# Second block's heads in pairs on array tiles, columns of the modulation by transposes, last normalisation shared with ScalarE

## The chip, the cores and the metric

The kernel runs on one core of one Trainium2 chip. The metric is device time in microseconds (us), from the first to the last instruction with what the runtime adds around them. All data is float32. Where full speed is wanted, a float32 value is split into a leading part in the fp32r format ("lead") and the difference ("rest"), and a product is made as lead·lead + lead·rest + rest·lead, so three fast matmuls stand for one float32 product. Small products (attention, transposes) use plain float32 matmuls.

## What is computed

A first block (one Hyena-and-attention layer, one mLSTM layer), then a second block of two layers, each a mixer of three branches and an MLP, and a last RMS norm. For 256 tokens of width 1024. The parts that this change touches, cut to what matters:

```python
def adaln(cond, w_mod, b_mod):                       # first block
    m = jax.nn.silu(cond) @ w_mod + b_mod            # shift, scale, gate
h = rms_norm(x, g_pre) * (1 + scale) + shift

# second block, per layer: 8 heads of width 64 twice (MoBA branch and MLA branch), causal
s = q @ k.T * scale          # MLA: 96 features per head, MoBA: 64
p = softmax(s + causal)
o = p @ v                    # v: 64 features per head
# retention branch: 4 heads, 64 features for q and k, 128 for v
o = (q @ k.T * decay) @ v;  o = group_norm(o) * silu(gate)
# each branch: y += sigmoid(gate_b) * (o_b @ w_branch_b), then @ w_out, then the MLP
out = rms_norm(x, final_norm)
```

With 256 tokens the block choice of MoBA has one block only, so that both branches are plain causal attention here.

## The kernel before

The program is one instruction stream per engine. Every piece of work is a generator that yields a place (a number) ahead of each step, and `merge` puts the steps of all generators of an engine in order of these places. So the order is written by hand: one unit of place is one quarter-unit of weights, 12 matmuls of 512 columns in the second block's input projection. Each engine then runs its stream strictly in order and waits on semaphores.

**Weights.** All weights stream through a ring of four 1 MB slots. ScalarE makes the lead (`take_lead`, L325), VectorE the rest (`take_rest`, L144), and `Dense` multiplies (`split_matmul`, L171, and `joined_matmul`, L164 and L165). These matmuls fill TensorE; everything else is slipped between them.

**Attention of the second block** (`CausalAttention`, used four times: MoBA and MLA, in two layers). It goes head by head, one head every 1.4 places: `scores` makes two float32 matmuls (128 and 256 columns; L2566, L2567), `maxima` adds the mask and takes the row maxima on VectorE (L2578, L2581), `exps` is on ScalarE (L2591), `turns` transposes three 128x128 blocks of the probabilities (L2602), `copies` brings them to SBUF (ScalarE, L2612), `values` multiplies with the 128x128 probabilities as weights and 64 columns of v moving (L2623 to L2625), and `outs` divides by the row sums on VectorE (L2634, L2638). In MoBA a head's q and k lie on 64 partitions, the even heads on the lower half and the odd ones on the upper. In MLA they lie on 96.
The results of all three branches go to `oa` (tokens on partitions) and are turned again by `o_turn` in six blocks of four transposes, each block with a copy on ScalarE and a subtraction on VectorE into `oT`.

**Retention** has the same shape, with four heads of 64 features (L2670, L2671), and `group_norm` normalises its output on VectorE (L3025 to L3037) while MLA runs.

**Modulation** (`Mods`). Conditions times `w_mod` are made on four column tiles of 32 (L1008), which leaves partial sums on partitions 0, 1, 32, 33, 64, 65, 96 and 97. For shift and scale, `turns` multiplies each 128 columns of these rows by a selection matrix of two columns (`sel`, L1046), which sums the four parts and turns them at once. VectorE adds the biases from PSUM (L1071 to L1073). There are four such chunks of 512 columns for each of the two layers of the first block; the first four stand ahead of the first projection, where TensorE also runs the Hyena filter (L846, L940).

**The end** (`Finish`). The last product comes in four groups. Each is added to x (L3214), squared on ScalarE, multiplied by the gain (L3251) and scaled by the reciprocal root (L3258, L3261) on VectorE, and stored by four DMAs from SyncE's queue (L3267).

## Time and profile before

| | us |
|---|---|
| median of three runs | 1815.84 |
| lowest and highest run | 1814.3, 1822.47 |
| the profiled execution | 1814.24 |
| its span, first to last instruction | 1812.4 |
| TensorE busy | 1763.4 (97%) |
| VectorE busy | 1157.7 (64%) |
| ScalarE busy | 916.4 (51%) |
| mean granted clock | 0.994 |

1.84 us of the profiled execution lie around its span. The span falls into the first block (to about 925 us), the mixer of the second block's first layer (about 925 to 1130), its output and MLP, the second layer (mixer about 1395 to 1567), its MLP, and an end of some 7 us after the last matmul. TensorE's busy time counts overlapping matmuls; so what a piece costs is read from starts: the distance between the start of the matmul before it and the start of the one after it. A plain fp32r matmul of 512 columns starts every 0.23 us, one of 416 columns every 0.19 us.

### The profile page before, as it was taken

How to read it: one execution, taken by the hardware profiler on the slowest of the kernel's cores; microseconds unless marked ns; L12 is line 12 of the kernel's file. 1: busy time of each engine (PE TensorE's matmuls, PEld its weight loads, DVE VectorE, ACT ScalarE, POOL GpSimd, SP SyncE). 2: the span in 40 equal slices, each digit the busy share in tenths (PEclk: the TensorE clock that was granted, in tenths of full speed). 3: DMA queues.
4: the chain of work that ended last, by engine and by line, in shares of the span. 5: the costliest groups of instructions: out<-in, count | busy, mean ns of one | idle time of the engine just before them, and what ended most of it. 6: DMA issues, size and time to landing. Idle time of an engine off the chain costs nothing. (4 is left out here: it accounts for less than half of the span.)

```text
span 1812.4 us, 23043 instructions
## 1 busy us (share of the span) xinstructions
PE 1763.4 (97%) x8648; PEld 1428.6 (79%) x8648; DVE 1157.7 (64%) x2095; ACT 916.4 (51%) x1484; POOL 47.1 (3%) x67
## 2 busy tenths in 40 slices
PE   9999999999998999999999999999999999999998
PEld 4867788777787877777778788788887888778886
DVE  6563466688428457766766675777646666577844
ACT  4333444333336356656656456367535546547743
POOL 0000000000000010000100010000000002000000
PEclk9999999999999999999999999999999999999999
DMA  9556211221335334443544444556555344455562
GB/s 340 190 180 209 93 58 60 69 71 66 122 114 177 114 110 144 146 151 116 171 133 145 140 145 147 185 169 196 192 188 172 125 146 138 166 167 186 186 212 78
DMA packets 116165, 268.27 MB, mean 148 GB/s; under 512 B 5388, under 2 KB 9773, under 8 KB 115864
## 3 DMA queue, kind: packets, MB, share of 16 engines
q1 hardware_dynamic: 111528, 252.52, 42.4%
q0 software_dynamic: 3696, 11.98, 2.1%
q10 hardware_dynamic: 832, 2.30, 0.3%
q8 instruction: 69, 1.13, 0.2%
q14 instruction: 40, 0.33, 0.1%
HBM read 265.66 MB, written 1.13 MB: 147 GB/s over the span
## 5 line engine op out<-in xcount | busy, mean ns | idle before, releaser
L144 DVE TENSOR_TENSOR qw_rest<-weights,qw_lead 128x1024 fp32r<-128x1024 f32 (+2 forms) x428 | 518.6, 1217 | 404.0 <-ACT qw_lead L325 400.7
L325 ACT ACTIVATE qw_lead<-weights 128x1024 fp32r<-128x1024 f32 (+2 forms) x428 | 446.7, 1048 | 468.2 <-PE psum L171 433.8
L171 PE MATMUL psum<-qw_lead,b_h_pair 128*128 128x512 f32 (+1 forms) x960 | 323.1, 400 | 1.7 <-ACT b_mqk L2925 0.9
L171 PEld LDWEIGHTS psum<-qw_lead,b_h_pair 128*128 128x128 f32 x960 | 180.6, 188 | 41.7 <-issue 5.0
L171 PE MATMUL psum<-qw_rest,b_h_pair 128*128 128x512 f32 (+1 forms) x480 | 186.2, 388 | 0.0
L164 PE MATMUL psum<-b_h_pair,qw_lead 128*128 128x512 f32 x512 | 178.3, 393 | 2.0 <-DVE b_h_pair L662 2.0
L171 PE MATMUL psum<-e_h_lead,qw_lead 128*128 128x512 f32 x320 | 141.1, 441 | 1.8 <-DVE e_qT L1441 1.4
L165 PE MATMUL psum<-b_h_pair,qw_rest 128*128 128x256 f32 x512 | 142.6, 279 | 0.0
L171 PE MATMUL psum<-e_h_lead,qw_rest 128*128 128x512 f32 x320 | 125.8, 393 | 0.0
L171 PE MATMUL psum<-e_h_rest,qw_lead 128*128 128x512 f32 x320 | 125.0, 390 | 0.0
L164 PEld LDWEIGHTS psum<-b_h_pair,qw_lead 128*128 128x128 f32 x512 | 95.9, 187 | 24.3 <-DVE b_h_pair L662 2.9
L171 PE MATMUL psum<-qw_lead,o_h_lead 128*128 128x512 f32 x256 | 110.2, 430 | 3.1 <-PEq L118 3.1
L171 PEld LDWEIGHTS psum<-qw_rest,b_h_pair 128*128 128x128 f32 x480 | 90.7, 189 | 14.8
L171 PE MATMUL psum<-qw_lead,o_h_rest 128*128 128x512 f32 x256 | 101.0, 395 | 0.0
L171 PE MATMUL psum<-qw_rest,o_h_lead 128*128 128x512 f32 x256 | 101.0, 395 | 0.0
L171 PE MATMUL psum<-qw_lead,b_upT_rest 128*128 128x512 f32 x256 | 99.6, 389 | 0.0
L171 PE MATMUL psum<-qw_rest,b_upT_lead 128*128 128x512 f32 x256 | 99.6, 389 | 0.0
L171 PE MATMUL psum<-qw_lead,b_upT_lead 128*128 128x512 f32 x256 | 99.6, 389 | 0.0
L165 PEld LDWEIGHTS psum<-b_h_pair,qw_rest 128*128 128x128 f32 x512 | 96.5, 188 | 0.0
L171 PE MATMUL psum<-qw_lead,e_h_lead 128*128 128x512 f32 x224 | 88.5, 395 | 1.1 <-DVE e_qT L1979 1.1
L171 PE MATMUL psum<-qw_lead,e_h_rest 128*128 128x512 f32 x224 | 87.2, 389 | 0.0
L171 PE MATMUL psum<-qw_rest,e_h_lead 128*128 128x512 f32 x224 | 87.2, 389 | 0.0
(485 smaller groups left out, 3102.5 us busy)
## 6 DMA issues: line engine op xcount, KB each, us to landing
weights<-in_w_in SPq DMA_DIRECT2D x48, 1024.0 KB, 5.1
weights<-in_o_w_in SPq DMA_DIRECT2D x32, 1024.0 KB, 5.4
weights<-in_w_mlp_up SPq DMA_DIRECT2D x32, 1024.0 KB, 5.5
weights<-in_w_mlp_down SPq DMA_DIRECT2D x32, 1024.0 KB, 4.9
weights<-in_e_w_in SPq DMA_DIRECT2D x26, 1024.0 KB, 5.1
weights<-in_w_mod SPq DMA_DIRECT2D x24, 1024.0 KB, 7.3
weights<-in_e_w_out SPq DMA_DIRECT2D x8, 1024.0 KB, 4.9
weights<-in_o_w_out SPq DMA_DIRECT2D x8, 1024.0 KB, 4.8
```

What stands on the lines that cost most here:

```text
L144: return eng.tensor_tensor(self.rest[at], src, self.lead[at].bitcast(F32), ALU.subtract)
L164: nc.tensor.matmul(out, lhs[0], pair, start=start, stop=False)
L165: return nc.tensor.matmul(out[:, 0:lead.shape[1]], lhs[1], lead, start=False, stop=stop)
L171: mm = nc.tensor.matmul(out, l, r, start=start and i == 0, stop=stop and i == 2)
L325: self.core.nc.scalar.activation(self.buf.lead[self.at(u)], self.raw(u), ACT.Copy).then_inc(self.lead_ready, 1)
```

## The change

It has six parts.

1. `CausalAttention` works on pairs of heads, one pair every 2.8 places. The scores of both heads are issued alternately, 128 columns of each and then 256 of each. In MoBA the two heads lie on different 64-row halves of the array. In MLA (96 rows) they can't.
2. The probabilities are divided by their sum before the transposes: a new step `norms` on VectorE (L2618, L2621: a reciprocal and two multiplications of 128 and 256 columns per head). `turns` now waits for it.
3. `values` takes v (64 columns) as weights and the turned probabilities as moving data (256 and 128 columns), with the two heads on different 64-column halves of the array. The result comes out already turned; a ScalarE copy and a VectorE subtraction per pair (`leads`, `rests`) write it to `oT`. `o_turn` is left with the two blocks of retention.
4. Retention's scores also go in pairs on 64-row halves. The steps of `group_norm` and of the rotations stand at other places in VectorE's order, between other work.
5. `Mods` turns shift and scale rows with plain transposes (L1051), and a new reduction on VectorE (L1073, `summed`) adds the four parts. The next chunk's transposes now wait for `summed` of the chunk before, since the four transposes fill the bank.
6. `Finish` gives the first of four scalings to ScalarE (`first_scale`) and the third store to ScalarE's queue, and its steps stand in another order.

Beside these, the masks' load for the mLSTM waits for its gate weights' load on GpSimd, and unused semaphores are gone. Before is marked -, after +.

```diff
     def scores(self, pe):
-            if j >= 2:
-                pe.wait_ge(self.negmax, j - 1)
-            q, k, _, _ = self.heads[j]
-            b = self.banks[j % 2]
-            nc.tensor.matmul(ps[:, b, 0:P], q(0), k(P), start=True, stop=True)
-            nc.tensor.matmul(ps[:, b, P:3 * P], q(1), k(2 * P), start=True, stop=True).then_inc(self.scored, 1)
+            else:
+                pe.wait_ge(self.negmax, 2 * j)
+            for t, (lo, hi) in enumerate(((0, P), (P, 3 * P))):
+                for i in range(2):
+                    q, k, _ = self.heads[2 * j + i]
+                    mm = nc.tensor.matmul(ps[:, self.banks[i], lo:hi], q(t), k((t + 1) * P), start=True, stop=True)
+                    if t:
+                        mm.then_inc(self.scored, 1)
...
+    def norms(self, dve):
+        nc = self.core.nc
+        for j, i, h, at in self.singles(1.3, 0.3):
+            yield at
+            dve.wait_ge(self.exped, 2 * h + 2)
+            self.core.dve_chain(dve, nc.vector.reciprocal(self.rec[:, 2 * h:2 * h + 2], self.tot[:, 2 * h:2 * h + 2]))
+            p = self.prob[:, i, :]
+            for t, (lo, hi) in enumerate(((0, P), (P, 3 * P))):
+                last = nc.vector.tensor_tensor(p[:, lo:hi], p[:, lo:hi], self.rec[:, 2 * h + t:2 * h + t + 1].broadcast_to([P, hi - lo]), ALU.mult)
+            last.then_inc(self.prob_ready, 1)
+
     def turns(self, pe):
-        for j, at in self.times(1.6):
+        for j, i, h, at in self.singles(1.8, 0.45):
             yield at
-            pe.wait_ge(self.exped, 2 * j + 2)
+            pe.wait_ge(self.prob_ready, h + 1)
...
     def values(self, pe):
-            nc.tensor.matmul(ps[:, b, 0:w], pt[:, 0:P], v(0), start=True, stop=True)
-            nc.tensor.matmul(ps[:, b, w:2 * w], pt[:, P:2 * P], v(0), start=True, stop=False)
-            nc.tensor.matmul(ps[:, b, w:2 * w], pt[:, 2 * P:3 * P], v(1), start=False, stop=True).then_inc(self.valued, 1)
+            for t in range(LT):
+                for i in range(2):
+                    v, pt = self.heads[2 * j + i][2], self.probT[:, i, :]
+                    mm = nc.tensor.matmul(ps[64 * i:64 * i + 64, self.banks[3], t * P:2 * P], v(t), pt[:, 2 * t * P:(2 + t) * P], start=(t == 0), stop=(t == 1))
+            mm.then_inc(self.valued, 1)
...
-    o_turn = split_turn(T + "ot_", r.oT, blocks, [branch_at - 5.0 + 0.8 * n for n in range(6)], (3, 4, 5, 6), o_ready, lambda pe: mla.wait_all(pe))
+    o_turn = split_turn(T + "ot_", r.low, blocks, [branch_at - 1.8 + 0.8 * n for n in range(2)], (3, 4), o_ready, lambda pe: mla.wait_all(pe))
...
-    gn_at = t0 + 26.4 + 3 * 1.2 + 2.5
+    gn_at = mla_start + 1.65
...
 # Mods.turns, Mods.takes
-                done = sum(2 for z in self.chunks[:i] if z[1] in (2, 3))
+                done = sum(1 for z in self.chunks[:i] if z[1] < 4)
                 if done:
-                    pe.wait_ge(self.mod_ready, done)
+                    pe.wait_ge(self.summed, done)
                 for b in range(4):
-                    o = (4 * j + b) * 2
-                    mm = nc.tensor.matmul(ps[:, self.spread_bank[0], o:o + 2], self.rows[i % len(self.rows)][:, b * P:(b + 1) * P], sel, start=True, stop=True)
+                    mm = nc.tensor.transpose(ps[:, self.spread_bank[0], b * P:(b + 1) * P], self.rows[i % len(self.rows)][:, b * P:(b + 1) * P], self.core.ident[:])
...
+            nc.vector.tensor_reduce(self.columns[:, 8 * j:8 * j + 8].rearrange("p (b s) -> p b s", s=2), parts, AX.X, ALU.add).then_inc(self.summed, 1)
...
 # Finish
+    def first_scale(self, act):
+        yield self.at - 0.2
+        act.wait_ge(self.rec_ready, 1)
+        act.wait_ge(self.gained, 1)
+        o = self.room.out[:, 0, 0:BANK]
+        self.core.nc.scalar.activation(o, o, ACT.Identity, scale=self.rec[:, 0:1]).then_inc(self.first_ready, 1)
```

TensorE in MoBA of the first layer, before: the values of one head and the scores of another (L171 is the projection, `ga` holds probabilities, `b_gates` turned ones, `hT` q and k, `b_mv` v):

```order
L171 MATMUL psum<-qw_lead,b_h_pair 128x416
L2623 MATMUL psum<-b_mv,b_gates 128x64
L2624 MATMUL psum<-b_mv,b_gates 128x64
L2625 MATMUL psum<-b_mv,b_gates 128x64
L2566 MATMUL psum<-hT 128x128
L2567 MATMUL psum<-hT 128x256
L171 MATMUL psum<-qw_lead,b_h_pair 128x512
```

The same place after: scores of a pair, half a quarter-unit of projection, and values of the pair before.

```order
L171 MATMUL psum<-qw_lead,b_h_pair 128x416
L2584 MATMUL psum<-hT 128x128 x2
L2584 MATMUL psum<-hT 128x256 x2
L171 MATMUL psum<-qw_lead,b_h_pair 128x512
L171 MATMUL psum<-qw_rest,b_h_pair 128x512
L171 MATMUL psum<-qw_lead,b_h_pair 128x512 x2
L171 MATMUL psum<-qw_rest,b_h_pair 128x512
L171 MATMUL psum<-qw_lead,b_h_pair 128x512
L2655 MATMUL psum<-b_gates,b_mv 64x256 x2
L2655 MATMUL psum<-b_gates,b_mv 64x128 x2
```

Six matmuls of 64 columns for two heads became four on half the array's columns, 768 columns in all, and the four score matmuls of two heads stand together.

VectorE in MLA of the first layer, before: the maxima of the second head after the group norm's first steps.

```order
L3025 TENSOR_REDUCE small<-b_oa 128x8
L3026 TENSOR_SCALAR small<-small 128x8
L3028 TENSOR_TENSOR b_oa<-b_oa,small 128x2x512
L144 TENSOR_TENSOR qw_rest<-weights,qw_lead 128x1024
L3030 TENSOR_TENSOR hT<-b_oa 128x1024
L2578 ISA ga,small<-psum,ga 128x128
```

After: the norms of the second head of the first pair, five steps of the group norm, and then the maxima of the next pair (L2597).

```order
L2618 RECIPROCAL small<-small 128x2
L2621 TENSOR_TENSOR ga<-ga,small 128x128
L2621 TENSOR_TENSOR ga<-ga,small 128x256
L3061 TENSOR_REDUCE small<-b_oa 128x8
L3062 TENSOR_SCALAR small<-small 128x8
L3064 TENSOR_TENSOR b_oa<-b_oa,small 128x1024
L2827 TENSOR_SCALAR b_gates<-psum,small 128x512
L144 TENSOR_TENSOR qw_rest<-weights,qw_lead 128x1024
L3066 TENSOR_TENSOR hT<-b_oa 128x1024
L3068 TENSOR_REDUCE small<-hT 128x8
L3069 TENSOR_SCALAR small<-small 128x8
L2597 ISA ga,small<-psum,ga 128x128
```

The whole group norm up to its variance now stands between two pairs.

VectorE at the start of the kernel, after, with the waits: the reduction of the first chunk (L1073) stands behind the four scalings of x.

```order
L1172 RECIPROCAL small<-small 128x4 [waits in_rooted]
L1174 TENSOR_SCALAR x_res<-x_res,small 128x1024 [waits dve_step]
L1174 TENSOR_SCALAR x_res<-x_res,small 128x1024 x3
L1073 TENSOR_REDUCE small<-psum 128x8 [waits m0_spread]
L964 COPY hy_F<-psum 128x512 [waits hy_F_done]
L1073 TENSOR_REDUCE small<-psum 128x8 [waits m0_spread]
```

And TensorE there, after; before, the second chunk waited for `m0_rows_out` only.

```order
L1051 MATMUL psum<-ident,e_qT 128x128 [waits m0_rows_out]
L1051 MATMUL psum<-ident,e_qT 128x128 x3
L943 MATMUL psum<-hT,hy_dft 128x512 [waits hy_filt_out]
L943 MATMUL psum<-hT,hy_dft 128x512
L1051 MATMUL psum<-ident,e_qT 128x128 [waits m0_summed,m0_rows_out]
```

TensorE's second set of transposes waits for VectorE's first reduction, which stands behind four operations of 1024 columns.

## Rows read from the trace of the kernel before

**Rows 1.** The page, busy time of TensorE, share of the span, instructions.

```profile
PE 1763.4 (97%) x8648; PEld 1428.6 (79%) x8648; DVE 1157.7 (64%) x2095; ACT 916.4 (51%) x1484; POOL 47.1 (3%) x67
```

**Rows 2.** Busy time of each engine in a stretch of MLA.

```profile
core 0: us, PE busy (x) PEld busy (x) DVE busy (x) ACT busy (x) POOL busy (x), PEclk, DMA share, GB/s
1060.00:1080.00 20.00, 20.00 (x111) 17.11 (x110) 16.36 (x38) 13.65 (x29) 7.02 (x4) 1.00 0.46 139
```

**Rows 3.** TensorE in order of time: start, duration, a MoBA head's scores.

```profile
972.16 0.35 PE L171 MATMUL psum<-qw_lead,b_h_pair 128*128 128x416 f32 x1
972.45 0.48 PE L2566 MATMUL psum<-hT 64*128 64x128 f32 x2
...
973.30 0.46 PE L171 MATMUL psum<-qw_lead,b_h_pair 128*128 128x416 f32 x1
973.59 0.35 PE L171 MATMUL psum<-qw_rest,b_h_pair 128*128 128x416 f32 x1
```

**Rows 4.** TensorE in order of time: an MLA head's values, then another's scores.

```profile
1060.72 0.33 PE L2623 MATMUL psum<-b_mqk,b_gates 128*128 128x64 f32 x2
...
1061.33 0.44 PE L2566 MATMUL psum<-b_mT 96*128 96x128 f32 x2
...
1062.28 0.39 PE L171 MATMUL psum<-qw_rest,b_h_pair 128*128 128x512 f32 x1
```

**Rows 5.** TensorE in order of time: one block of `o_turn`.

```profile
1112.37 0.60 PE L721 MATMUL psum<-ident,b_oa 128*128 128x128 f32 x4
...
1113.04 0.39 PE L171 MATMUL psum<-qw_rest,b_h_pair 128*128 128x512 f32 x1
```

**Rows 6.** TensorE in order of time: the start of the kernel.

```profile
17.23 1.07 PE L1008 MATMUL psum<-weights,cond 128*32 128x512 f32 x8
18.23 1.99 PE L940 MATMUL psum<-hT,hy_dft 128*128 128x512 f32 x4
...
32.19 1.05 PE L1046 MATMUL psum<-small,e_qT 128*128 128x2 f32 x8 [0.57 <-ACT e_qT L1019]
33.11 1.96 PE L940 MATMUL psum<-hT,hy_dft 128*128 128x512 f32 x4
```

**Rows 7.** VectorE in order of time: the start of the kernel.

```profile
31.90 2.74 DVE L1165 TENSOR_SCALAR x_res<-x_res,small 128x1024 f32<-128x1024 f32 x4
```

**Rows 8.** VectorE in order of time: MLA of the first layer.

```profile
1054.04 1.22 DVE L3025 TENSOR_REDUCE small<-b_oa 128x8 f32<-128x1024 f32 x1
...
1063.02 0.16 DVE L2634 RECIPROCAL small<-small 128x2 f32<-128x2 f32 x1
1063.21 0.29 DVE L2638 TENSOR_TENSOR b_oa<-psum,small 128x128 f32<-128x128 f32 x1
1063.42 0.28 DVE L2578 CUSTOM_DVE_ANT_0 ga<-psum,ga 128x128 f32<-128x128 f32 x1
...
1063.62 0.42 DVE L2578 CUSTOM_DVE_ANT_0 ga<-psum,ga 128x256 f32<-128x256 f32 x1
1063.97 0.09 DVE L2578 DVE_READ_ACCUMULATOR2_ANT small<- 128x1 f32 x1
```

**Rows 9.** The two costliest lines of VectorE and ScalarE: busy, mean ns.

```profile
L144 DVE TENSOR_TENSOR qw_rest<-weights,qw_lead 128x1024 fp32r<-128x1024 f32 (+2 forms) x428 | 518.6, 1217 | 404.0 <-ACT qw_lead L325 400.7
L325 ACT ACTIVATE qw_lead<-weights 128x1024 fp32r<-128x1024 f32 (+2 forms) x428 | 446.7, 1048 | 468.2 <-PE psum L171 433.8
```

**Rows 10.** Who waited for whom: total us, times, longest.

```profile
PE psum L2602 <- ACT ga L2591: 0.3, 1, 0.3
```

**Rows 11.** VectorE in order of time: the end.

```profile
1805.19 0.15 DVE L3258 RECIPROCAL small<-small 128x1 f32<-128x1 f32 x1
1805.38 0.48 DVE L3261 TENSOR_SCALAR hT<-hT,small 128x512 f32<-128x512 f32 x1
1805.78 0.74 DVE L3214 SCALAR_TENSOR_TENSOR x_res<-psum,small,x_res 128x512 f32<-128x512 f32 x1
...
1808.84 0.88 DVE L3261 TENSOR_SCALAR hT<-hT,small 128x512 f32<-128x512 f32 x2
```

248 lines of the change are left out of this document (139 added, 109 removed).

## Prediction

> **What bounds the kernel now.** I read the page's busy times first: TensorE is busy for 1763.4 of 1812.4 us, VectorE for 1157.7 [rows 1]. In the mixers of the second block, where most of the change lies, TensorE has no gap in stretches of 20 us, even where VectorE is busiest, at 16.36 of 20 us [rows 2]. So time comes off only where TensorE's stream gets shorter, and a cost on another engine counts only where TensorE then waits. The waits say that this hardly happens now: in the four attentions the transposes of the probabilities waited once for the exponentials, for 0.3 us [rows 10]. Next I read TensorE's order of time around each small piece. A piece costs the distance between the starts of the projection matmuls on either side, less the ordinary distance of these (0.19 us at 416 columns, 0.23 us at 512). All sums are made against the profiled execution's 1814.24 us; the median of the three runs, 1815.84, is 1.6 us above it, and I forecast near the profiled level.
>
> **Scores on row halves.** One MoBA head's two score products take 973.59 - 972.16 = 1.43 us with a 0.19 us step at either end, so about 1.05 us [rows 3]. MoBA has 8 heads in each of two layers, so 8 pairs. If the two halves run side by side, a pair costs what a head costs now, and 8 x 1.05 = 8.4 us go. Bounds: if the halves take turns, only one entry and exit per pair goes, 2 x 1.05 - (1.05 + 0.85) = 0.2 us, as 973.30 - 972.45 = 0.85 is a head without them [rows 3]; that is 1.6 us. If the pair is as well filled as a 96-row head, 62.28 - 61.33 - 0.23 = 0.72 us [rows 4], it is 8 x 1.38 = 11.0 us. I take 8.4. Retention's scores have the same rows, columns and form; 8 heads or 4 pairs give 4.2 us (0.8 to 5.5). MLA's scores keep their columns and don't overlap: nothing.
> No row shows two row halves at once. The nearest are the column tiles of the modulation: four products of 512 columns on four 32-column tiles took 1.00 us until the next matmul started, while two full-array products of that length have 1.99 us [rows 6]. So tiles do run side by side on this chip, in one direction of the array at least. The Trainium skill says the same of both directions (TensorE: Matmul & The Clock Gate, Part 3: Packing small matmuls).
>
> **Values on column halves.** A head's six instructions (three products) take 61.33 - 60.72 = 0.61 us now, 1.22 us a pair [rows 4]. The new form streams 384 columns per head. A float32 product of 384 columns in all costs 0.72 us in MLA's scores [rows 4], so a pair side by side costs about that, and up to 1.05 us if a half-array group has the overhead that the MoBA scores show [rows 3]. I take 0.80: 16 pairs x 0.42 = 6.7 us. Bounds: 16 x 0.17 = 2.7 and 16 x 0.50 = 8.0 us. If they took turns, a pair would cost 1.4 us and the sum would lose 3 us, but the four column tiles speak against that [rows 6].
> A rule of the Trainium skill speaks against this part: a change of the tiling mode drains TensorE (TensorEngine Tiling (Array Packing), Key Properties). The trace bears it out as the difference of 1.05 to 0.72 us between the half-row and the 96-row scores; by the rule alone values would cost 1.05 a pair, which is the lower bound above.
>
> **Fewer transposes.** A block of four costs 1113.04 - 1112.37 - 0.23 = 0.44 us [rows 5]. Four blocks go in each layer: 8 x 0.44 = 3.5 us. Their ScalarE and VectorE work isn't saved, it moves into `leads` and `rests`.
>
> **Modulation.** A chunk's four two-column products take 33.11 - 32.19 = 0.92 us [rows 6], four transposes 0.44 [rows 5], so 0.48 us less per chunk. For the four chunks of the second set, which lie within the projection, that is 1.9 us. In the first set the new wait decides. Before, the second chunk starts at 32.19. Now it needs the first chunk's reduction, and that stands in VectorE's order behind the four scalings of x, which run from 31.90 to 34.64 [rows 7]; with some 0.2 us for a small reduction it starts at about 34.85. It is 2.66 us late and 0.48 shorter: 2.2 us lost, and everything behind it on TensorE moves (filter, transposes of x, the next products), as no gap follows until the first projection. Two more chunks give back 0.96. The set costs 1.2 us; all modulation gains 0.7 (bounds -2 and +3). The reductions themselves are a few tenths on VectorE and hidden by the 8 quarter-units between chunks.
>
> **What the norms add to VectorE.** Now a head's reciprocal and division are 0.19 + 0.21 = 0.40 us from start to start; the new step is a reciprocal, 128 and 256 columns, 0.19 + 0.21 + 0.35 = 0.75 [rows 8]. 32 heads make +11 us, hidden if TensorE doesn't wait. But the chain from scores to transposes gets longer. For an ordinary pair TensorE has 24 projection matmuls (5.5 us), its scores and the values of the pair before, some 7.7 us, ahead of the first transpose. VectorE has ahead of its norm: two maxima (0.77 each), one or two weight rests (1.14 each), a result's rest (0.35) that itself waits for the values, and the norm: it is done some 0.8 us before it is due. The tight place is MLA's second pair, behind the group norm. From the first scores of MLA on, VectorE has 1.5 (maxima) + 1.5 (norms) + 1.14 (rest) + six steps of the group norm (four of 1024 columns at about 1.2, two small: 5.1) + a projection output and a weight rest (1.8) + maxima, weight rest, result (2.3) + maxima and norm (1.5), 14.8 us in all [rows 8, 9]; TensorE comes to that transpose after 4.6 places, 12.7 + 2.6 + 1.4 = 16.7 us. With the waits for the first scores and for exponentials within, that leaves next to nothing. I take one turn late by a norm, 0.75 us, in each of the four attentions: 3 us lost. Bounds: 0, and half a norm for each of 32 turns, 12 us.
>
> **The end.** The fourth addition moves ahead of the first scaling, from 1805.78 to about 1805.3 [rows 11], but ScalarE now has the first scaling ahead of its last two squares, which gives 0.1 or 0.2 us of it back, and the last two scalings stay. The third store leaves SyncE's queue. I take 0.7 us (0 to 1.0).
>
> **Costs that I set at nothing.** The later group norm: GpSimd, which takes it up, then still waits for the gates. The masks' later load: it is issued far ahead of its reader. Rotations in pieces: the same instructions.
>
> **Sum.** 8.4 + 4.2 + 6.7 + 3.5 + 0.7 + 0.7 - 3.0 = 21.2 us, so 1793.0 us.
>
> **Rivals.**
> A. Row halves take turns. Scores then give 1.6 + 0.8 instead of 12.6 us: 1814.2 - 11.0 = 1803.2. For it: no row of before has two row halves in flight. Against it: the column tiles.
> B. VectorE late more often: some 10 to 17 us of new waits, so that most of the gain comes back, 1803 to 1810, with 1807 in the middle. For it: 16.36 of 20 us in rows 2, and the exact fit at the second MLA pair. Against it: VectorE waits for 404 us of the kernel on the line that it spends most time in [rows 9], so it catches up in a pair or two.
> C. Slower: VectorE becomes the bound of the attentions. If each of the 32 transposes of a head waits for its norm and one weight rest queued ahead (0.75 + 1.14 us), 60 us are added and 24 saved, 1850 us. It turns slower than now from 0.76 us of waiting per turn (24.2 / 32).
> D. The change doesn't save on the values, since the halves serialise or each small product pays a full load: 6.7 turns to -3, 1803.
>
> **How the numbers follow.** Forecast 0.57, A 0.12, B 0.14, C 0.06, D 0.05, and 0.06 for a part worth more than I took. The range reaches from 1784 (scores, values and retention at their better bounds and no new wait: 21.2 + 2.6 + 1.3 + 1.3 + 3.0 = 29.4 us) to 1809, which holds A, D and most of B. About 0.5% (9 us) is what a measurement of this kernel can tell from no change, so the line is at 1805: the forecast, what is better than it, A and D lie below it, 0.80, B within 0.5%, 0.14, and C above, 0.06.
>
> **What would show it.** TensorE: MoBA score groups with both heads started within a few hundredths and about 1.05 us for the group; values groups of 0.8 us; 16 transposes fewer per layer; a gap of about 3.5 us near 31 us, ended by the reduction. VectorE: about 1170 us busy. The waits: transposes of the probabilities waiting for L2621, a few times, 3 us together. Wrong would be: score groups of 1.9 us (A), many waits for L2621 or for L144 (B, C), values groups of 1.4 us (D).

## Result and profile after

| | before | after |
|---|---|---|
| median of the runs | 1815.84 | 1804.62 |
| lowest and highest | 1814.3, 1822.47 | 1803.35, 1807.37 |
| profiled execution, its span | 1814.24, 1812.4 | 1805.85, 1803.7 |
| ratio after to before, 95% interval | | 0.994, 0.9929 to 0.9951 |

The changed kernel is faster by 11.2 us (medians), 0.6%. The forecast was 1793.0, a gain of 21.2 us on the profiled execution before, so about half of it came. The measured time alone doesn't tell which rival is right: A (1803.2), D (1803) and the lower end of B (1803 to 1810) lie near it. All times are in us.

The page of the changed kernel, busy time of the two engines of [rows 1]. TensorE has 22 us less to do, near the 24 us that the forecast's terms make without the new waits, and VectorE 12 us more (some 1170 were forecast):

```profile
PE 1741.3 (97%) x8520; PEld 1395.5 (77%) x8520; DVE 1169.8 (65%) x2142; ACT 918.9 (51%) x1493; POOL 47.0 (3%) x67
```

TensorE in order of time, first layer: one pair of MoBA scores (what a single head was in [rows 3]), and one pair of values alone ([rows 4] has one head's):

```profile
968.39 0.34 PE L171 MATMUL psum<-qw_lead,b_h_pair 128*128 128x416 f32 x1
968.67 0.93 PE L2584 MATMUL psum<-hT 64*128 64x128 f32 x8
969.52 0.46 PE L171 MATMUL psum<-qw_lead,b_h_pair 128*128 128x416 f32 x1
969.82 0.35 PE L171 MATMUL psum<-qw_rest,b_h_pair 128*128 128x416 f32 x1
...
1090.89 0.40 PE L171 MATMUL psum<-qw_lead,b_h_pair 128*128 128x512 f32 x1
1091.22 0.87 PE L2655 MATMUL psum<-b_gates,b_mqk 128*64 128x256 f32 x8
1092.02 0.50 PE L171 MATMUL psum<-qw_lead,b_h_pair 128*128 128x512 f32 x1
1092.35 0.40 PE L171 MATMUL psum<-qw_rest,b_h_pair 128*128 128x512 f32 x1
```

969.82 - 968.39 less two steps of 0.19 is 1.05 for two heads: the row halves run side by side. 1092.35 - 1090.89 less two steps of 0.23 is 1.00 for the values of two heads, where 0.80 was forecast and 1.33 was paid before (0.66 to 0.67 a head, read in the same way).

Who waited for whom on TensorE (total, times, longest), the lines that are new or longer than before. Before had L2602 with 0.3 [rows 10]; L171 for the gates' copies had 2.0, once, and L721 (now L724) 0.9, twice:

```profile
PE psum L2632 <- DVE ga L2621: 6.5, 7, 1.3
...
PE psum L171 <- ACT b_gates L2826: 3.3, 3, 2.0
...
PE psum L1051 <- DVE small L1073: 2.4, 1, 2.4
...
PE psum L724 <- ACT hT L2825: 1.7, 2, 0.8
...
PE psum L2632 <- ACT b_gates L2642: 0.7, 3, 0.2
```

A wait isn't all that a stop costs. In MLA of the first layer a group of transposes costs 0.34; the one that waited 0.67 costs 1.22, the one that waited 1.30 costs 1.86. So each stop has 0.2 us on top.

### The profile page after: what moved, and what is told of

It is laid out like the page before. It is cut to its first block and busy times, and to the rows that moved or that the text cites. A ratio compares the mean times of both kernels' runs of the same rounds, so it can differ in the third digit from the quotient of the medians.

```text
span 1803.7 us, 22788 instructions
## 1 busy us (share of the span) xinstructions
PE 1741.3 (97%) x8520; PEld 1395.5 (77%) x8520; DVE 1169.8 (65%) x2142; ACT 918.9 (51%) x1493; POOL 47.0 (3%) x67
## 5 line engine op out<-in xcount | busy, mean ns | idle before, releaser
L171 PE MATMUL psum<-qw_lead,b_h_pair 128*128 128x512 f32 (+1 forms) x960 | 320.5, 399 | 3.2 <-ACT b_gates L2826 1.4
L171 PEld LDWEIGHTS psum<-qw_lead,b_h_pair 128*128 128x128 f32 x960 | 181.0, 189 | 43.7 <-issue 3.7
L171 PE MATMUL psum<-qw_rest,b_h_pair 128*128 128x512 f32 (+1 forms) x480 | 186.5, 389 | 0.0
L171 PE MATMUL psum<-e_h_lead,qw_lead 128*128 128x512 f32 x320 | 141.1, 441 | 1.8 <-DVE e_qT L1450 1.4
L171 PE MATMUL psum<-e_h_lead,qw_rest 128*128 128x512 f32 x320 | 125.8, 393 | 0.0
L171 PE MATMUL psum<-e_h_rest,qw_lead 128*128 128x512 f32 x320 | 124.9, 390 | 0.0
L171 PE MATMUL psum<-qw_lead,o_h_lead 128*128 128x512 f32 x256 | 109.6, 428 | 3.1 <-PEq L118 3.1
L171 PEld LDWEIGHTS psum<-qw_rest,b_h_pair 128*128 128x128 f32 x480 | 90.7, 189 | 14.9
L171 PE MATMUL psum<-qw_lead,o_h_rest 128*128 128x512 f32 x256 | 100.6, 393 | 0.0
L171 PE MATMUL psum<-qw_rest,o_h_lead 128*128 128x512 f32 x256 | 100.5, 392 | 0.0
L171 PE MATMUL psum<-qw_lead,b_upT_rest 128*128 128x512 f32 x256 | 99.6, 389 | 0.0
L171 PE MATMUL psum<-qw_rest,b_upT_lead 128*128 128x512 f32 x256 | 99.6, 389 | 0.0
L171 PE MATMUL psum<-qw_lead,b_upT_lead 128*128 128x512 f32 x256 | 99.6, 389 | 0.0
L171 PE MATMUL psum<-qw_lead,e_h_lead 128*128 128x512 f32 x224 | 88.5, 395 | 1.1 <-DVE e_qT L1988 1.1
L171 PE MATMUL psum<-qw_lead,e_h_rest 128*128 128x512 f32 x224 | 87.2, 389 | 0.0
L171 PE MATMUL psum<-qw_rest,e_h_lead 128*128 128x512 f32 x224 | 87.2, 389 | 0.0
```

Of the source, the lines that this page charges most:

```text
L171: mm = nc.tensor.matmul(out, l, r, start=start and i == 0, stop=stop and i == 2)
```

## Experiments

The table holds every kernel's median, its ratio to the kernel before (95% interval), and four lengths from its one profiled execution: the start of the first projection matmul; the first layer's MoBA stage, from its first scores to the first retention scores; and the MLA stage of both layers, from its first scores to the first branch matmul. The lengths tell causes apart that the medians can't: where a kernel leaves a stage alone, its length comes back within 0.1 (MoBA 57.41 in before and 57.43 in `e_mods`). The first projection doesn't: it lies between 53.3 and 55.7 in the kernels that differ from the changed one only behind it. Three lengths also hold a fall of the granted clock to 0.50 behind a wait, which cost 1.6 each time: MoBA of `e_low_place`, and MLA of `e_lnexp` in both layers.

| kernel | median | ratio | first projection | MoBA | MLA, layers 1, 2 |
|---|---|---|---|---|---|
| before | 1815.84 | | 50.92 | 57.41 | 76.46, 77.44 |
| after | 1804.62 | 0.994 | 53.55 | 53.71 | 76.67, 77.61 |
| e_pairs | 1806.57 | 0.9943 (0.9929, 0.9958) | 51.35 | 54.35 | 76.45, 77.47 |
| e_mods | 1817.61 | 1.0004 (0.9994, 1.0015) | 55.09 | 57.43 | 76.51, 77.45 |
| e_no_norm | 1802.13 | 0.9921 (0.9906, 0.9936) | 55.67 | 52.50 | 75.79, 76.74 |
| e_norm_twice | 1815.46 | 0.999 (0.9981, 0.9998) | 54.43 | 56.31 | 79.09, 80.07 |
| e_low_place | 1807.96 | 0.9957 (0.9941, 0.9972) | 54.41 | 55.59 | 76.70, 77.68 |
| e_lnexp | 1812.03 | 0.9976 (0.9966, 0.9986) | 54.68 | 53.63 | 78.92, 80.12 |
| e_no_norm_lnexp | 1806.7 | 0.995 (0.9935, 0.9965) | 53.93 | 52.64 | 77.25, 78.21 |
| e_no_root | 1804.95 | 0.9934 (0.9921, 0.9948) | 55.07 | 51.81 | 76.68, 77.64 |
| e_early_tables | 1803.66 | 0.9929 (0.9914, 0.9943) | 53.30 | 52.27 | 76.72, 77.67 |
| e_values_one_half | 1812.7 | 0.9981 (0.9973, 0.9989) | 54.11 | 55.79 | 78.19, 79.11 |
| e_reduce | 1802.43 | 0.9926 (0.9912, 0.994) | 50.21 | 53.71 | 76.71, 77.68 |
| e_norm_first | 1805.76 | 0.994 (0.9928, 0.9952) | 54.73 | 53.25 | 76.57, 77.53 |
| e_gn_late | 1805.42 | 0.994 (0.9928, 0.9952) | 54.27 | 53.69 | 76.65, 77.57 |
| e_finish_old | 1805.06 | 0.9939 (0.9927, 0.9951) | 55.29 | 53.66 | 76.68, 77.63 |
| e_best1 | 1798.73 | 0.9909 (0.9894, 0.9924) | 50.29 | 51.39 | 76.33, 78.12 |
| e_best3 | 1795.78 | 0.9889 (0.9874, 0.9904) | 54.34 | 51.40 | 74.86, 76.58 |
| e_best4 | 1795.15 | 0.9886 (0.987, 0.9903) | 51.08 | 51.41 | 74.88, 76.58 |

### Are the parts worth what was forecast?

My first theory was that the parts on TensorE are right and the missing 10 us are transposes that wait for VectorE. `e_pairs` is the kernel before, with the paired scores alone:

```diff
-            nc.tensor.matmul(ps[:, b, 0:P], q(0), k(P), start=True, stop=True)
-            nc.tensor.matmul(ps[:, b, P:3 * P], q(1), k(2 * P), start=True, stop=True).then_inc(self.scored, 1)
+            for t, (lo, hi) in enumerate(((0, P), (P, 3 * P))):
+                for i in range(2):
+                    q, k, _, _ = self.heads[2 * n + i]
+                    mm = nc.tensor.matmul(ps[:, self.banks[i], lo:hi], q(t), k((t + 1) * P), start=True, stop=True)
```

> The kernel before with one part of the change alone: MoBA's and retention's scores in pairs on 64-row halves. The prediction put 8.4 + 4.2 = 12.6 us on it, so 1803.2 against 1815.8. The groups of the changed kernel read 1.05 us a pair as forecast, so I expect 11 to 13 us. Rival: a pair frees TensorE but the head behind waits for its maxima or its decay, since two heads come at once (VectorE then has two heads' maxima in a row, the second head's exponentials wait); then 7 to 9 us, 1807 to 1809.

Ratio 0.9943, 10.3 us by it, between the two forecasts. A pair costs 1.05, as forecast; retention's stage loses 1.98 per layer (2.1 forecast). MoBA gains 3.06 in the first layer instead of 4.2, since a value product of the old form waits 2.02 us for the division of the head before; in the kernel before it waited 1.04 at the same place. VectorE and, last, TensorE there:

```profile
994.72 1.22 DVE L2529 TENSOR_TENSOR b_gates<-hT,x_res 128x1024 f32<-128x1024 f32 x1
...
998.51 0.29 DVE L2654 TENSOR_TENSOR b_oa<-psum,small 128x128 f32<-128x128 f32 x1
998.95 0.41 PE L2639 MATMUL psum<-b_mv,b_gates 128*128 128x64 f32 x2 [2.02 <-DVE b_oa L2654]
```

The division stands behind the four steps of a rotation (L2529 to L2532, 994.72 to 998.41), and not behind maxima. So row halves side by side are shown; the rival is right that a stop takes some of it back, and not in its reason.

`e_values_one_half` is the changed kernel, with both heads' values on one column half:

```diff
-            for t in range(LT):
-                for i in range(2):
+            for i in range(2):
+                for t in range(LT):
                     v, pt = self.heads[2 * j + i][2], self.probT[:, i, :]
-                    mm = nc.tensor.matmul(ps[64 * i:64 * i + 64, self.banks[3], t * P:2 * P], v(t), pt[:, 2 * t * P:(2 + t) * P], start=(t == 0), stop=(t == 1))
+                    mm = nc.tensor.matmul(ps[0:64, self.banks[3], SEQ * i + t * P:SEQ * i + 2 * P], v(t), pt[:, 2 * t * P:(2 + t) * P], start=(t == 0), stop=(t == 1))
```

> The changed kernel with the value products of both heads of a pair on the same 64-column half, one head after the other, into different columns of the bank (the odd heads' outputs then don't reach their rows, that part of the computation is wrong on this run): same number of products, columns and weights, no two side by side. The groups of two heads take 1.00 us in the changed kernel. If the halves overlap, the columns alone (768 of float32, 1.05 us for 384 in a half-row group, 0.72 in MLA's) make this 1.6 to 1.9 us a pair, 16 pairs, 10 to 14 us more, 1814 to 1819. Rival D of the prediction (the halves take turns or each product pays its load anyway): the same 1.00 us, 1804 to 1806.

A pair costs 1.64 to 1.66 instead of 1.00, and the kernel 7 to 8 us more, less than the 10 to 14 expected. So the column halves do overlap, for 0.65 us of each pair, and rival D is out. (16 x 0.65 is 10.4. The stages grow by 2.1 in MoBA and 1.5 in MLA, 7.1 in both layers; part of the rest is waits that are shorter, as the transposes behind now come later: 4.7 us for L2621 instead of 6.5.)

### The start

`e_mods` is the kernel before with the new `Mods` alone, `e_reduce` the changed kernel with one step elsewhere (x's norm stands at places -14.95 and -14.6):

```diff
-            yield self.turn_at[i] + self.lags[2] - self.lags[1]
+            yield self.first_sum if i == 0 and self.first_sum else self.turn_at[i] + self.lags[2] - self.lags[1]
...
+    mods0.first_sum = -14.96
```

> The kernel before with one part of the change alone: the modulation's shift and scale by plain transposes and a reduction. The prediction gives it 0.7 us of gain (second set 1.9 less, first set 1.2 more), 1815.1. The changed kernel's trace has the second set at -1.9, and the first set at +2.6 to the first projection, but its start was also disturbed by a wait for a load and by the clock. If the loss of 2.6 belongs to the change, this kernel is 0.7 us slower than before, 1816.5; if it is the run's, it is 0.7 to 1.8 faster, 1814 to 1815.1.

> The changed kernel with one step at another place: the first chunk's reduction of the modulation goes ahead of VectorE's normalisation of x instead of behind its four scalings. In the kernels with the changed modulation TensorE stops for 4.6 to 4.9 us there (L1051 waits for L1073), in the matmuls behind the stop the four of L943 take 3.6 instead of 1.9 us, and the first projection comes at 55.1 to 55.7 against 50.9 before. Theory (the wait and the clock behind it cost 4 us): first projection at about 50 to 51, 4 to 5 us less than the changed kernel, 1800 to 1801. Rival (x's scalings bound the start anyway, since TensorE's transposes of x need them all): TensorE stops there instead, 1 to 2 us less, 1802.6 to 1803.6.

`e_mods` isn't faster, 1.0004: its first projection comes 4.2 us later than before, and the four chunks of the second set give 1.9 back. TensorE in order of time in `e_no_norm` (same start), and the busy times of engines in two stretches of it (the column before DMA's share is the granted clock, PEclk):

```profile
28.78 0.66 PE L1051 MATMUL psum<-ident,e_qT 128*128 128x128 f32 x4
29.27 1.88 PE L943 MATMUL psum<-hT,hy_dft 128*128 128x512 f32 x4
35.75 1.09 PE L1051 MATMUL psum<-ident,e_qT 128*128 128x128 f32 x4 [4.60 <-DVE small L1073]
36.63 3.62 PE L943 MATMUL psum<-hT,hy_dft 128*128 128x512 f32 x4
```

```profile
core 0: us, PE busy (x) PEld busy (x) DVE busy (x) ACT busy (x) POOL busy (x), PEclk, DMA share, GB/s
28.00:32.00 4.00, 3.15 (x16) 1.07 (x8) 0.17 (x1) 3.63 (x8) 0.00 (x0) 1.00 1.05 388
...
36.00:40.00 4.00, 4.00 (x8) 1.88 (x8) 1.10 (x8) 0.00 (x0) 0.00 (x0) 0.50 0.45 164
```

The transposes are done at 29.3, but the reduction stands in VectorE's order behind x's norm, which waits for ScalarE's squares of x. After the stop of 4.60 the granted clock is 0.50, that is 1.2 of 2.4 GHz, and the same four matmuls take 3.62 instead of 1.88. The changed kernel's own profiled run had a wait of only 2.44 and kept its clock behind it. TensorE came late to it there, since it had waited 1.71 us for a load (L849) at 12.83 and had a granted clock of 0.50 from 15.0 to 21.5. With the reduction ahead of x's norm the first projection comes at 50.21 and the median is 2.2 us lower, less than the theory's 4 to 5: TensorE now waits 1.7 us at the same chunk for ScalarE's copy, which stands behind the same squares.

`e_best4` took that copy away too (with all other remedies, below):

> The version with all remedies, and the copy of the modulation's second chunk made by VectorE, ahead of x's norm, instead of by ScalarE behind x's squares and root. Theory (x's scalings, which end at 34.6 us, are the third in the same row and TensorE's transposes of x need all four): the 1.7 us wait at the second chunk goes, TensorE then stops about as long ahead of the transposes of x, the first projection stays at about 50 us and the time within 1 us of the last version, 1795 to 1796.5. Rival (the copy was the last thing in the way): the first projection comes 1.7 us earlier, 1794.

```profile
31.52 0.60 PE L1052 MATMUL psum<-ident,e_qT 128*128 128x128 f32 x4
31.96 1.88 PE L943 MATMUL psum<-hT,hy_dft 128*128 128x512 f32 x4
35.48 1.09 PE L1186 MATMUL psum<-ident,x_res 128*128 128x128 f32 x8 [1.64 <-DVE x_res L1175]
```

As expected: the stop moves to the transposes of x, 1.64, and the first projection stays near, at 51.08. The start is bound by x's load and norm. `e_best3` shows the load: it has the early reduction too, but the third of ScalarE's four squares, which waits for the load of x in both, starts at 29.82 instead of 27.48 in `e_reduce`. TensorE waited 4.36 for ScalarE's copy, the granted clock fell to 0.50 behind it, and the first projection came at 54.34. So the place of the reduction doesn't take the stop away in every execution.

### MoBA: who makes the transposes wait?

`e_no_norm` and `e_norm_twice` take VectorE's new work away and double it (the diff of the first; the second repeats the loop over `t`):

```diff
-        self.vector, self.scalar = (self.maxima, self.norms, self.rests), (self.exps, self.copies, self.leads)
+        self.vector, self.scalar = (self.maxima, self.rests), (self.exps, self.copies, self.leads)
...
-            pe.wait_ge(self.prob_ready, h + 1)
+            pe.wait_ge(self.exped, 2 * h + 2)
```

> The changed kernel without its step `norms`: the transposes wait for the exponentials, the probabilities are not divided by their sums (that part of the computation is left out), and VectorE has 0.9 us less to do for each of 32 heads, some 28 us in all. The changed kernel took 1804.6. My theory now: the missing 10 us of the forecast lie mainly in transposes that wait for VectorE (17.4 us of PE's and the weight loader's idle time stand under L2632 and L2621, over about ten turns, and a turn that waits costs its wait and about 0.5 us more). Then this kernel takes 8 to 10 us less than the changed one, 1795 to 1797. Rival 1, the prediction's own figure: the waits cost 3 us, so 1801 to 1802. Rival 2: TensorE stops elsewhere for the same VectorE work (projection groups, value groups), so that nothing is gained, 1804.

> The changed kernel with the two multiplications of each head made twice (the probabilities are divided by their sum two times, so the attention outputs are not the reference's): VectorE has about 0.7 us more per head, 22 us in all, on the chain ahead of each transpose. If the transposes wait because VectorE is late, most heads become late ones: each head that already waits adds 0.7 us, and others begin to wait at 0.5 us for the stop itself; 32 heads, some 10 to 20 us more, 1815 to 1825. Rival (only a few places are tight, the others have slack of a microsecond or more): 10 waiting turns by 0.7 us, 7 us, 1811 to 1813.

My theory fell with the first. Without norms only 3.4 us come back by the ratio (0.9921 against 0.994; 2.5 by the medians), because the transposes then wait for ScalarE. Its waits, first line:

```profile
PE psum L2632 <- ACT b_gates L2642: 5.2, 8, 1.1
```

Twice the norms cost 9 us by the ratio (11 by the medians), with 16 waits of 16.8 us in all, as its theory said. So VectorE matters, but it isn't the only one that is late. ScalarE of the changed kernel in order of time, at MoBA's second pair, and below it VectorE's norm for it (it is ready for the transpose at 986.08, which waited 0.85):

```profile
980.95 0.39 ACT L2662 ACTIVATE b_oT_lead<-psum 128x256 fp32r<-128x256 f32 x1 [2.13 <-PE psum L2655]
981.35 1.28 ACT L2941 ACT_TABLE_LOAD   x1
982.65 0.21 ACT L2941 ACTIVATE small<-small 128x4 f32<-128x4 f32 x1
982.87 1.28 ACT L2610 ACT_TABLE_LOAD   x1
984.17 0.40 ACT L2610 ACTIVATE ga<-ga,small 128x128 f32<-128x128 f32 x1
```

```profile
985.19 0.17 DVE L2618 RECIPROCAL small<-small 128x2 f32<-128x2 f32 x1 [1.92 <-ACT ga L2610]
985.39 0.63 DVE L2621 TENSOR_TENSOR ga<-ga,small 128x128 f32<-128x128 f32 x2
```

VectorE had been idle for 1.92 us. The exponentials were late because ScalarE loaded a table for the square root of `low_root` and another to come back: 2.8 us with the root. Four kernels test this: the root at its old place (1.0 instead of 0.55), the roots as exp(-0.5 ln x), that without norms, and copies in place of the roots; `e_early_tables` puts the loads into ScalarE's idle time:

```diff
-        yield low_at + 0.55
+        yield low_at + 0.4
         act.wait_ge(low_meaned, 1)
         nc.scalar.activation(r.low_stat[1], r.low_stat[0], ACT.Sqrt).then_inc(low_rooted, 1)
+        yield low_at + 0.6
+        nc.scalar.activation(core.small[:, 60:61], core.small[:, 60:61], ACT.Exp)
```

> The changed kernel with one line back at its old place: ScalarE's root of the MLA inputs' norm (`low_root`, place 0.55) at place 1.0 again. In the changed kernel this root brings two loads of activation tables (1.28 us each, 2.8 us with the root) between the maxima and the exponentials of MoBA's second pair, and the norms and transposes behind them are those that wait at 986.08 and 989.08. Theory (ScalarE's tables are what the waits named after VectorE's L2621 hide): both waits of MoBA go in each layer, so 2.5 to 4 us less than the changed kernel, 1800.6 to 1802. Rival (VectorE is loaded in MoBA whatever ScalarE does): the waits stay, within 1 us of 1804.6.

> The changed kernel with both square roots inside the attentions (MLA inputs' norm and group norm) made as exp(-0.5 ln x), whose two functions can share one table with the exponentials, so that no table is loaded between them (four loads of 1.28 us fewer per layer). Theory (ScalarE's tables): the waits at 986, 989 and 1076 of the first layer and 1420 and 1509 of the second go; with about 0.5 us for each stop saved too, 4 to 6 us less than the changed kernel, 1798.6 to 1800.6. What stays by this theory is the transpose at 1067.33 (1.30 us), whose norm stood behind a weight rest that waited for ScalarE's lead. Rival (VectorE's own work): same waits, 1803 to 1805.

> Both at once: without the norms (the probabilities are not divided, that part of the computation is left out) and with the roots as exp(-0.5 ln x). Leaving out the norms alone gave 1802.1, since the transposes then waited 5.2 us for ScalarE's copies (L2642) in place of 7 us for the norms. Theory (behind both names stands ScalarE, late by its table loads): now neither is late and nearly nothing waits, 1795 to 1798. Rival (a transpose group has only one PSUM bank, so the second head's transposes wait for the first head's copy whatever ScalarE has before it): the waits for copies stay, 1800 to 1802.

> The changed kernel with plain copies in place of the two square roots inside the attentions (MLA inputs' norm and group norm; that part of the computation is left out), so that ScalarE loads no table there: four loads of 1.28 us fewer per layer are possible, and this time the trace can show it, which the exp(-0.5 ln x) form did not (it loaded a table for each of its two functions, back to back, and the MLA stage became 2.3 us longer per layer). Theory (ScalarE's loads are behind most waits): waits of the transposes fall from 7.2 to about 1.5 us (the one at 1067 stays in each layer), 4 to 6 us less than the changed kernel, 1798.6 to 1800.6. Rival: VectorE's own load makes them, 1803 to 1805.

> The changed kernel with ScalarE's table loads at better places and nothing left out: the root of MLA's inputs goes ahead of the copy that waits for the first pair's values (ScalarE is idle for 2.1 us there), and an exponential of a single element behind each root brings the table back before the maxima are ready. Theory: the exponentials of MoBA's second pair and MLA's third come 1.3 us earlier each, and about half of the transposes' waits go: 2 to 3.5 us less than the changed kernel, 1801 to 1802.6. Rival: the loads only move ahead of other work that is waited for (copies of probabilities, leads), 1804 to 1806.

- `e_low_place`: in the first layer the waits for norms in MoBA go, but the loads now stand ahead of a copy of probabilities, and one transpose waits 2.3 us for it (L2642). MoBA is 1.9 longer, of which 1.6 is the clock behind that wait (the row below) and 0.3 the stop. In the second layer one wait for a norm stays, of 1.56, and MoBA is 1.0 longer (55.44 instead of 54.40) with the clock at 1.00. So neither forecast was right: what waits for the loads changes with their place, and the changed kernel's place is no worse than the old one.

```profile
992.00:994.00 2.00, 2.00 (x9) 1.25 (x10) 0.00 (x0) 0.87 (x2) 0.00 (x0) 0.50 0.80 197
```

- `e_lnexp`: I had wrongly taken it that the logarithm brings a table that also holds the exponential. ScalarE loads one for each, back to back. This became a test in the other direction: in MLA, where one load became two ahead of a copy, a transpose waits 2.81 us instead of 1.30 and the stage is 2.3 and 2.5 us longer. Of each, 1.6 is the granted clock behind that wait (0.52 from 1072 to 1074, 0.54 from 1509 to 1511) and 1.5 the longer stop, and 0.9 came off at the next transpose, whose wait is gone. These are the rows, ScalarE at the group norm's root:

```profile
1066.20 1.28 ACT L3077 ACT_TABLE_LOAD   x1
1067.50 0.21 ACT L3077 ACTIVATE small<-small 128x8 f32<-128x8 f32 x1
1067.72 1.28 ACT L3078 ACT_TABLE_LOAD   x1
1069.02 0.21 ACT L3078 ACTIVATE small<-small 128x8 f32<-128x8 f32 x1
1069.13 0.47 ACT L2642 ACTIVATE b_gates<-psum 128x384 f32<-128x384 f32 x1
```

- `e_no_norm_lnexp` has the same two loads, and 8.0 us of waits for L2642; against `e_no_norm` MLA is 1.5 longer per layer, and no clock fell in it. It doesn't tell its theory and rival apart.
- `e_no_root`, with no loads between the exponentials, settles MoBA: 51.81 instead of 53.71 (53.15 instead of 54.40 in the second layer), and no transpose of MoBA waits for a norm. In MLA nothing changes (76.68), against my expectation.
- `e_early_tables`, with everything computed, gets MoBA to 52.27 (53.09).

The medians of the last two are 1804.95 and 1803.66, hardly below the changed kernel's. The ratios, 0.9934 and 0.9929, lie inside its interval or at its edge, so that the 1.3 to 1.9 us per MoBA stage are shown by the stage's length alone.

The Trainium skill (ScalarE: Activation LUTs, What ACT_TABLE_LOAD costs) gives 1.283 us for a load and 1.38 more for a drain at each switch. The load agrees with the rows. The drain isn't there: the first exponential starts 2.82 us after the first load, and 1.28 + 0.21 + 1.28 is 2.77.

### MLA: two causes, one behind the other

MLA gained nothing in either layer. Four pairs of values (0.33 each) and four blocks of `o_turn` (0.44 each) should take 3.1 us off it. New waits of the transposes took 2.7 of them, and a new wait of 0.68 for a gates' copy the rest (1101.15; `e_best3` still has one of 0.64). VectorE in order of time around its two waits, which ended at 1067.33 (1.30) and 1076.35 (0.67):

```profile
1063.40 0.63 DVE L2621 TENSOR_TENSOR ga<-ga,small 128x128 f32<-128x128 f32 x2
1065.31 1.22 DVE L144 TENSOR_TENSOR qw_rest<-weights,qw_lead 128x1024 fp32r<-128x1024 f32 x1 [1.28 <-ACT qw_lead L325]
1066.45 0.16 DVE L2618 RECIPROCAL small<-small 128x2 f32<-128x2 f32 x1
...
1073.98 0.60 DVE L2600 TENSOR_SCALAR small<-small 128x2 f32<-128x2 f32 x1
1074.49 0.15 DVE L2618 RECIPROCAL small<-small 128x2 f32<-128x2 f32 x1
1074.68 1.61 DVE L2621 TENSOR_TENSOR ga<-ga,small 128x128 f32<-128x128 f32 x2
```

The first norm stands behind a weight rest that itself waits 1.28 us for ScalarE, while its exponentials ended at 1064.3. The second is slow itself: 1.61 and 0.60 for operations that take 0.63 and 0.17 elsewhere. In that stretch GpSimd multiplies the group norm's output and adds to it. It did so for 7 us in the kernel before as well, but there the operation that took longer was a weight rest (2.14 instead of 1.22), and no transpose waited for it. GpSimd after; GpSimd and VectorE before:

```profile
1068.80 7.01 POOL L3087 TENSOR_TENSOR b_oa<-b_oa,x_res 128x512 f32<-128x512 f32 x4 [25.12 <-DVE b_oa L3073]
...
1067.08 7.10 POOL L3051 TENSOR_TENSOR b_oa<-b_oa,x_res 128x512 f32<-128x512 f32 x4 [18.55 <-DVE b_oa L3037]
1070.91 2.14 DVE L144 TENSOR_TENSOR qw_rest<-weights,qw_lead 128x1024 fp32r<-128x1024 f32 x1 [0.29 <-ACT qw_lead L325]
```

Two kernels test one each. First `e_norm_first`, in `norms`, then `e_gn_late`, in `group_norm` and `gn_root`:

```diff
-        for j, i, h, at in self.singles(1.3, 0.3):
+        for j, i, h, at in self.singles(1.3, 0.15):
```

```diff
-        yield gn_at + 3.3
+        yield mla_start + 10.3
         dve.wait_ge(gn_rooted, 1)
...
-        yield gn_at + 2.5
+        yield mla_start + 9.8
         act.wait_ge(gn_meaned, 1)
```

> The changed kernel with the norm of each pair's second head 0.15 places earlier on VectorE. That swaps it with a weight rest in four places, one in each attention, one of them the place of the 1.30 us wait in the MLA stage of each layer: there the norm stood behind a rest that waited 1.28 us for ScalarE's lead, while its exponentials were long done. Theory (an in-order queue, not VectorE's load): the waits at 1067 and 1500 go and 1.5 us come off each layer's MLA stage, 3 us in all, 1801.6. Rival: the transposes then wait for ScalarE's copy of the first head in place of it (it did so when the norms were left out, 0.74 us there), 1803 to 1804.6.

> The changed kernel with the group norm's root, its last multiplication and so GpSimd's work behind it moved from the second MLA pair to behind the last pair's exponentials. In the changed kernel GpSimd's four tensor operations run from 1068.7 to 1075.7, and in that stretch VectorE's small operations take longer: 0.60 us for a scaling of the maxima (0.17 else) and 1.61 for the two multiplications of a norm (0.63 else), 1.4 us in all ahead of the transpose that waited 0.65 us. Theory (the two engines disturb each other, and a table load goes from the attention too): that wait goes, the operations are back at 0.17 and 0.63, and the MLA stage is 0.9 us or more shorter per layer, 1802 to 1803. Rival: the wait is VectorE's load of rests and maxima anyway and stays, 1804 to 1805; a further one, that the group norm is then late for the branches, shows as a wait of its transposes.

`e_norm_first`: the transpose waits exactly as long, for somebody else:

```profile
1067.85 0.52 PE L2632 MATMUL psum<-ident,ga 128*128 128x128 f32 x3 [1.30 <-ACT b_gates L2642]
```

There is one bank for turned probabilities, so that the second head's transposes need the first head's copy, and that stood behind the table load of the group norm's root. Taking the norm's lateness away (here) or the root away (`e_no_root`) leaves the wait at 1.30; each hides the other. (Without any norms, in `e_no_norm`, it is 0.74, for the copy.)

`e_gn_late`: the operations of VectorE are back to normal at the same pair, and the wait of 0.67 is gone. The stage gains nothing, since the table load is now at the last pair, where a transpose waits 0.63 for a copy. The slow operations go with GpSimd's work: in the mixers of both layers of before, the changed kernel, `e_no_norm`, `e_norm_first`, `e_gn_late`, `e_best3` and `e_best4`, every VectorE operation that took clearly longer than its like lay beside one of GpSimd's. Most of those beside it took their usual time: in the changed kernel's first layer 14 of 16.

```profile
1074.83 0.17 DVE L2600 TENSOR_SCALAR small<-small 128x2 f32<-128x2 f32 x1
1074.91 0.16 DVE L2618 RECIPROCAL small<-small 128x2 f32<-128x2 f32 x1
1075.10 0.62 DVE L2621 TENSOR_TENSOR ga<-ga,small 128x128 f32<-128x128 f32 x2
```

### All causes at once

`e_best1` has the early reduction, the tables of `e_early_tables`, norms with a per-partition scalar (0.35 instead of 0.42 for the 256 columns, less than was expected), and transposes, copies, values, `leads` and `rests` 0.3 places later. `e_best3` also has the norms of `e_norm_first` and the group norm of `e_gn_late`, so that the one-element exponential behind its root isn't needed. `e_best4` is that with the second chunk's copy on VectorE.

```diff
-                last = nc.vector.tensor_tensor(p[:, lo:hi], p[:, lo:hi], self.rec[:, 2 * h + t:2 * h + t + 1].broadcast_to([P, hi - lo]), ALU.mult)
+                last = nc.vector.tensor_scalar(p[:, lo:hi], p[:, lo:hi], self.rec[:, 2 * h + t:2 * h + t + 1], None, ALU.mult)
...
-        for j, i, h, at in self.singles(1.8, 0.45):
+        for j, i, h, at in self.singles(2.1, 0.45):
```

> The changed kernel with all remedies, nothing left out: the modulation's first reduction ahead of x's norm (1802.4 alone), the table loads at their better places, the norms' two multiplications with a per-partition scalar (0.25 us for 256 columns at L2936, against 0.41 for the form with two tensors), and the transposes, copies and values of each pair 0.3 places later. Theory: nothing of the transposes' waits is left, 2.3 us from the reduction and 5 to 7 from the waits, 1796 to 1798. Rival (later transposes only move the stop to the value products or to ScalarE's copies): 1800 to 1802.

> All remedies together, nothing left out: the first reduction early, the MLA inputs' root and the table behind it early, the group norm's root behind the last exponentials, norms with a per-partition scalar and ahead of the rests, transposes, copies and values 0.3 places later. The earlier set of remedies gave 1798.7 and left 4.6 us of waits in MLA behind the group norm's table load. Theory (the causes named are all there is): these go too, another 3 to 5 us, 1794 to 1796. Rival (the copies or values wait in their place): 1797 to 1799.

`e_best1` reached 1798.7; its rival was right that the stop moves: 4.6 us for ScalarE's copies, all in MLA. `e_best3` and `e_best4`, which compute everything, give 1795.8 and 1795.2, a ratio of 0.989, some 20 us below before and 9 below the changed kernel. Per layer MLA is 1.0 to 1.8 shorter than in the changed kernel and MoBA 2.3 in the first layer. No run tells how much of this is each remedy's. Of waits of the transposes `e_best4` has on TensorE:

```profile
PE psum L2634 <- ACT b_gates L2644: 1.6, 3, 0.7
```

### The end

`e_finish_old` is the changed kernel with the old `Finish`.

> The changed kernel with the old order and the old engines in the last normalisation. The prediction put 0.7 us (0 to 1.0) on that part. From the last product to the end the changed kernel takes 0.3 us less by its trace. I expect 0.3 to 0.7 us more than the changed kernel, 1804.9 to 1805.3, with the stretch from the last product to the end as the measure, since the medians can't tell this. Rival: no difference or a gain, 1804.2 or less.

From the start of the last product to the end of the span it takes 7.92, the changed kernel 7.55 and before 7.88. The part gives 0.3 to 0.4 us.

## Why the prediction was half right

Term by term, from the profiled executions (forecast, then measured; - is a gain):

| term | forecast | measured |
|---|---|---|
| MoBA scores | -8.4 | -8.4 (8 pairs at 1.05 instead of 2.10) |
| retention | -4.2 | -3.9 (stage -1.97 in each layer) |
| values | -6.7 | -5.3 to -6 (1.00 a pair alone and behind MLA scores, 0.81 behind MoBA scores, 1.33 before) |
| o_turn | -3.5 | -3.5 (2 blocks of 0.45 instead of 6, twice) |
| modulation, second set | -1.9 | -1.9 |
| modulation, first set | +1.2 | +2.6, and +4.2 in `e_mods` |
| end | -0.7 | -0.3 |
| new waits of transposes | +3.0 | +10.8 (with the stops) |
| not in the sum: projection waits for gates' copies | 0 | +1.4 |

The last but one is the excess of the groups with transposes, those of the probabilities at 0.34 each: 2.7 in MLA of either layer, 3.0 and 2.4 in MoBA. Against it stand 1.3 us for a value product's wait before, which is gone. With that and 1.6 us for a slower clock (below) the column gives -8.6, and the profiled execution is 8.4 below the one of before. (The medians are 11.2 apart.)

- **What bounds the kernel** held: TensorE's busy time fell by 22 us, and time was lost only where it waited or ran at the lower clock behind a wait.
- **Scores, retention, fewer transposes** were right in mechanism and size. Rival A is false.
- **Values**: right mechanism, mis-sized term. A pair costs 1.00, near the upper bound of 1.05 and not near the 0.80 that I took from the 96-row scores.
- **Modulation**: the right stop at the right place, forecast from the norm's time in before. Its price was wrong by the clock behind it (four matmuls in 3.62 instead of 1.88), and the length of the wait by when x arrives.
- **New waits** is the step that failed: 3.0 us were put into the sum and 10.8 came. I counted VectorE's work up to each transpose, and took one late turn per attention. At the one place where I had added everything up, MLA's second pair, the count held: TensorE came 16.9 us after the first scores (16.7 forecast), the first head's norm was just ready (1063.40 + 0.63), and its transposes, at 1064.09, didn't wait. The stop is at the pair's second head. Three things weren't in the count: ScalarE's table loads, which stand next to the exponentials and ahead of copies; a norm queued behind a rest that waits for ScalarE; and GpSimd's work, beside which some of VectorE's takes longer. The last is older than the change; what the change did is to put norms, which transposes wait for, where it runs. The later group norm, which I had set at nothing, moved GpSimd's work from 14.9 us behind MLA's first scores to 21.6; no run has it at its old place. The move of `low_root` wasn't in my list at all.
- **Rival B** (late more often, 10 to 17 us of new waits, 1803 to 1810) is what happened in size and in place. Its reason, VectorE's load, is one of four, so that its number is right in part by luck.
- **Rival C**, VectorE as the bound: `e_norm_twice` shows its slope, 9 us for 19 us more work (1188.7 busy instead of 1169.8), and 1815.5 is where the change is worth nothing.

What stays open: in the profiled executions of the changed kernel and of eight others the granted clock falls behind a wait of 1.98 us at the second layer's first branch matmul, and 1.6 us are lost; in before and nine others it doesn't, at the same wait. These are the two stretches behind it in the changed kernel, then the one in before:

```profile
1558.00:1560.00 2.00, 2.00 (x5) 1.54 (x6) 0.18 (x1) 0.00 (x0) 0.00 (x0) 0.50 0.15 15
1560.00:1562.00 2.00, 2.00 (x8) 1.61 (x7) 0.00 (x0) 0.00 (x0) 0.00 (x0) 0.71 1.02 396
```

```profile
1568.00:1570.00 2.00, 2.00 (x10) 1.64 (x9) 0.14 (x1) 0.00 (x0) 0.00 (x0) 1.00 0.19 26
```

I don't know what decides it. It moves single executions by as much as some parts of the change.

## What to carry to other kernels

When a step is put into a chain between two engines, list all that stands ahead of it on every engine of the chain, table loads and other engines' rests too; the name in a wait is only the last to arrive, and taking it away may show the next one with the same wait to the hundredth. Where two causes hide each other, neither is worth anything alone: `e_norm_first`, `e_gn_late` and `e_no_root` gave nothing in MLA, and the first two together with later transposes and the other remedies gave 1.8 us in the first layer. Judge such steps by the length of the stage, not by the median, and look at the granted clock inside the stage before you name a cause.

## What the runs showed of the hardware

- Column halves of 64: two float32 heads of 384 columns take 1.00 us side by side and 1.65 on one half. Row halves: 1.05 for two heads, the same as one head alone.
- After a wait of 4.60 us TensorE had a granted clock of 0.50 (36 to 40 us of `e_no_norm`); after 2.44 us in the changed kernel it stayed at 1.00. Waits of 2.27 (`e_low_place`) and 2.81 (`e_lnexp`, twice) were followed by 0.50 and cost 1.6 us each beyond the wait, and the same wait of 1.98 at the branches was in nine executions and wasn't in ten.
- GpSimd's float32 multiplications and additions beside VectorE: a scaling of 128x2 took 0.60 instead of 0.17, a norm's two multiplications 1.61 instead of 0.63, and a weight rest of 1024 columns 2.14 instead of 1.22. Most operations beside GpSimd's took their usual time.
- A logarithm and the exponential behind it cost two table loads of 1.28 us here. The Trainium skill (ScalarE: Activation LUTs, Table sets: the hidden batching unit) names a set that holds both, by which it would be one; the trace of `e_lnexp` has two.
